# A LayerNorm whose variance ScalarE finishes, and a last down product that takes one half of its columns first

## The chip, the cores and the metric

One core of one Trainium2 chip. The time is the device time of one execution in microseconds (us); the median of several runs is given. The profile shows one further execution.

## What is computed

256 tokens of width 1024 pass through two parts. The first has two layers; each is a feed-forward product with SwiGLU, a mixer (gated linear attention in the first layer, retention in the second) and a second SwiGLU, every one with a residual and a LayerNorm behind it. The second part has one layer: three kinds of attention whose results are gated and merged, a LayerNorm, a feed-forward product with a squared ReLU of hidden width 4096, and the last LayerNorm. That makes eight LayerNorms of this form (the second part's has the same mathematics):

```python
def layer_norm(x, g, b):
    mu = x.mean(-1, keepdims=True)
    var = jnp.square(x - mu).mean(-1, keepdims=True)
    return (x - mu) * lax.rsqrt(var + LN_EPS) * g + b      # LN_EPS = 1e-5

h = jnp.square(jax.nn.relu(x @ w_ff1))
x = layer_norm(alpha * x + h @ w_ff2, ln2_g, ln2_b)        # norm 8, the output
```

All data are fp32 and the products must be good to nearly fp32.

## The kernel before

Every fp32 product is made of three products of split operands: a value is a high part (rounded to the format that TensorE takes at one pass) and a low part (the rest). `three` (L1587 to L1598) issues high by high, high by low and low by high. The weights stream from HBM in tiles of 128 x 2048 through a ring of three slots: SyncE loads `raw`, ScalarE rounds it into `weights_hi` (`split_hi`, L436), VectorE subtracts to get `weights_lo` (`split_lo`, L919), TensorE uses both and gives the slot free (`weights_used`). All engines run programs written out by hand, each in its own order, tied by semaphores that count.

The tokens lie in two row blocks (tb = 0 and 1) of 128 rows. A down product ahead of a norm is summed in four PSUM banks, `acc[:, 2 * tb + half]`, one for each row block and half (512) of the columns. `block_product` (L1770 to L1799) makes the last tiles of such a product: all of row block 0, then all of row block 1. Within a row block it goes through its tiles s, the two chunks of 128 input rows in each tile (k) and the two halves; in the last tile it takes half 0 for both k before half 1. Before norm 8 (final=8, L2305) there are two tiles, so a row block has 24 matmuls, and of them the last 6 are for half 1 and the 6 ahead of these for half 0. When a half is complete it increments `acc_ready`, or `weights_used` for the last one.

Each norm works on these banks, one row block after the other:

- VectorE (`layer_norm`, L937 to L1006) evacuates a half with the residual added and sums it by row (`scalar_tensor_tensor`, L950), forms from half 0's sum a scaled mean (L955), evacuates half 1, and forms the gap of the sums, minus the mean, and `moment[3]` = gap squared minus the first second moment (L962, L963, L965, `surplus_ready`). Then it centres and multiplies by the gain (L970), waits for `rstd_ready`, and normalises the two halves (L975), each of which gives `xn_ready`.
- ScalarE (`layer_norm`, L450 to L474) squares each half about the scaled mean of half 0 and sums by row into `moment[0]` and `moment[1]` (L459), waits through `link` for each, and signals `first_moment` (half 0) and `var_ready` (half 1). In norms 1 to 7 it goes on with weight tiles and with rounding the transposed rows (L448).
- GpSimd (`layer_norm`, L350 to L361) waits for `surplus_ready` and `var_ready`, and in `inverse_root` (L325 to L330) makes moment[1] - moment[3] + eps with a tensor_scalar (L329) and its power of -1/2 with a tensor_tensor (L330). In norms 1 to 7 it also splits half of a weight tile (L338), makes the scaled residual (L348) and loads the next gains and shifts.
- TensorE transposes the normalised rows of norms 1 to 7 (`turn_rows`, L1606) in between its matmuls. Behind norm 8 comes only the output: SyncE stores four pieces (L310) as their `xn_ready` arrives.

VectorE does all of norm 8's row block 0 before anything of row block 1. Small tiles are declared first, then a filler of 24 floats a partition, `to_a_row`, then the large ones (L71 to L101).

Of the kernel before, what the change touches and what calls it, by code (L numbers as in the profile page):

```python
# [9 lines left out]
ALU = mybir.AluOpType  # L10
ACT = mybir.ActivationFunctionType
AX_X = mybir.AxisListType.X

P = 128
D = 1024
TOK = 256
TB = TOK // P
KC = D // P
NCOL = 512
# [18 lines left out]
LN_EPS, NORM_EPS = 1e-5, 1e-6  # L38
# [23 lines left out]
def build(nc, io):  # L62
    ctx = ExitStack()
    with ctx:
        def sb(name, shape, dt=F32, where=ctx):
            return where.enter_context(nc.sbuf_tensor(name, shape, dt))
# [4 lines left out]

        row_sum = sb("row_sum", [P, 2 * TB])
        minus_mean = sb("minus_mean", [P, TB])
        scaled_mean = sb("scaled_mean", [P, TB])
        moment = sb("moment", [P, TB, 4])
        ln_rstd = sb("ln_rstd", [P, TB])
        stats = sb("stats", [P, 8, 6])
# [237 lines left out]
        def _(pool):  # L315
            step = [0]

            def link(ins):
                step[0] += 1
                ins.then_inc(pool_step, 1)  # L320
                pool.wait_ge(pool_step, step[0])

            powers = [0]

            def inverse_root(out, var, scale, eps, n, op=ALU.mult):  # L325

                powers[0] += 1
                pool.wait_ge(var_ready, powers[0])
                link(nc.gpsimd.tensor_scalar(out, var, scale, eps, op, ALU.add))  # L329
                nc.gpsimd.tensor_tensor(out, out, minus_half[:, 0:n], ALU.pow).then_inc(rstd_ready, 1)  # L330

            link(nc.gpsimd.memset(minus_half[:, :], -0.5))

            def split_lo_piece(n, ln):
# [14 lines left out]

            def layer_norm(ln):  # L350
                for tb in range(TB):
                    pool.wait_ge(surplus_ready, 2 * (ln - 1) + tb + 1)
                    inverse_root(ln_rstd[:, tb:tb + 1], moment[:, tb, 1:2], moment[:, tb, 3:4], LN_EPS, 1, ALU.subtract)
                    if ln < 8 and tb == 0:
                        pool.wait_ge(xn_ready, 4 * (ln - 1) + 2)
                        split_lo_piece(LAYER_STARTS[ln] + 1, ln)
                if ln < 8:
                    pool.wait_ge(xn_ready, 4 * ln)
                    for tb in range(TB):
                        residual(tb, ALPHA if ln < 6 else ALPHA_2)  # L360
                    load_rows(ln + 1)  # L361
# [7 lines left out]
            pool.dma_start(cst[:, 1:, :], io["constants"][:, 1:, :]).then_inc(consts_loaded, 16)  # L369
            layer_norm(1)  # L370

            inverse_root(rstd[:, 0:4], g_ss[:, 0:4], 1.0 / GLA_DV, NORM_EPS, 4)
            inverse_root(rstd[:, 4:8], g_ss[:, 4:8], 1.0 / GLA_DV, NORM_EPS, 4)
            layer_norm(2)
            layer_norm(3)
            layer_norm(4)
# [16 lines left out]
                last.then_inc(gate_ready, 1)  # L393

            head_gain(0)
            inverse_root(rstd[:, 0:4], mv[:, 0:4, 1], 1.0, NORM_EPS, 4)
            head_gain(1)
            inverse_root(rstd[:, 4:8], mv[:, 4:8, 1], 1.0, NORM_EPS, 4)
            head_gain(2)
            head_gain(3)  # L400
            layer_norm(5)
# [14 lines left out]
        def _(act):  # L416
            step = [0]

            def link(ins):
                step[0] += 1  # L420
                ins.then_inc(act_step, 1)
                act.wait_ge(act_step, step[0])
# [29 lines left out]
            def layer_norm(ln, end):  # L452

                for tb in range(TB):
                    act.wait_ge(mean_ready, 2 * (ln - 1) + tb + 1)
                    for b in range(2):
                        cols = slice(b * NCOL, (b + 1) * NCOL)
                        act.wait_ge(evacuated, 4 * (ln - 1) + 2 * tb + b + 1)
                        link(nc.scalar.activation(squares[:, cols], xn[:, tb, cols], ACT.Square, bias=scaled_mean[:, tb:tb + 1],  # L459
                                                  scale=D ** -0.5, accum_out=moment[:, tb, b:b + 1]))  # L460
                        act.sem_inc(var_ready if b else first_moment, 1)  # L461
                    if ln == 8:
                        continue
                    if tb == 0 and ln != 2:
                        split_hi(end)
                    if tb == 0 and ln == 2:
                        split_hi(end + 1, first_piece=True)
                    if tb == 1:
                        split_hi(end + 2)
                    rows_hi(f"ln{ln}", tb, block_acc(tb))  # L470
                    if tb == 0 and ln != 2:
                        split_hi(end + 1, first_piece=True)
# [429 lines left out]
        def _(dve):  # L902
# [35 lines left out]
            def layer_norm(ln, end, scale):  # L938

                dve.wait_ge(rows_loaded, 32 * ln)  # L940
                for tb in range(TB):
                    dve.wait_ge(resid_ready, 2 * (ln - 1) + tb + 1)
                    held = ln == 2
                    for b in range(2):
                        cols = slice(b * NCOL, (b + 1) * NCOL)
                        if (tb, b) == (1, 1):
                            dve.wait_ge(weights_used, end)
                        else:
                            dve.wait_ge(acc_ready, 3 * (ln - 1) + 2 * tb + b + 1)
                        nc.vector.scalar_tensor_tensor(  # L950
                            out=xn[:, tb, cols], in0=acc[:, 2 * tb + b, :], scalar=scale, in1=resid[:, tb, cols],
                            op0=ALU.mult, op1=ALU.add, accum_out=row_sum[:, 2 * tb + b:2 * tb + b + 1]).then_inc(evacuated, 1)
                        if b == 0:
                            dve.wait_ge(evacuated, 4 * (ln - 1) + 2 * tb + 1)
                            nc.vector.tensor_scalar(scaled_mean[:, tb:tb + 1], row_sum[:, 2 * tb:2 * tb + 1], -2 * D ** -1.5, None,  # L955
                                                    ALU.mult).then_inc(mean_ready, 1)
                        if held and (tb, b) == (1, 0):
                            rows_lo("ln2", 0, block_acc(0), (0,))
                    dve.wait_ge(evacuated, 4 * (ln - 1) + 2 * tb + 2)
# [21 lines left out]
                    def split_lo_rest(cols):  # L981
                        s = slot_of(end + 1)
                        return nc.vector.tensor_tensor(w_lo[:, s, cols], raw[:, s, cols], w_hi[:, s, cols].bitcast(F32), ALU.subtract)
# [5 lines left out]
                    if held and tb == 1:  # L989
                        rows_lo("ln2", 0, block_acc(0), (1,))  # L990
                    elif ln < 8 and tb == 1:
                        dve.wait_ge(hi_split, end + 2)
                        split_lo_rest(slice(POOL_COLS, POOL_COLS + NCOL))
                    count[0] += 1
                    dve.wait_ge(rstd_ready, count[0])
                    normalise(halves[0])
# [590 lines left out]
        def _(pe):  # L1587
# [23 lines left out]
            def turn_normed(ln, tb):  # L1611
                return turn_rows(f"ln{ln}", xn, tb, block_acc(tb), xn_ready, lambda b: 4 * (ln - 1) + 2 * tb + b + 1)
# [157 lines left out]
            def block_product(n, ready, value, chunks, first=False, final=None, hooks={}):  # L1770

                tiles = len(chunks) // 2
                for tb in range(TB):
                    t = slice(tb * P, (tb + 1) * P)
                    for s in range(tiles):
                        slot = slot_of(n + s)
                        pe.wait_ge(lo_split, n + s + 1)  # L1780
                        pe.wait_ge(ready, value(tb, s))
                        order = [(k, half) for k in range(2) for half in range(2)]
                        if final is not None and s == tiles - 1:
                            order.sort(key=lambda at: at[1])
                        for k, half in order:
                            h_hi, h_lo, c = chunks[2 * s + k]
                            inner = (None, None)
                            if (tb, s, k, half) in hooks:
                                hooks[tb, s, k, half]()
                            if final is not None and final < 8 and (tb, s, k, half) == ((1, 1, 1, 1) if tiles == 2 else (1, 2, 0, 0)):  # L1790
                                inner = turn_normed(final, 0)
                            cols = slice(k * D + half * NCOL, k * D + (half + 1) * NCOL)
                            last = three(acc[:, 2 * tb + half, :], h_hi[:, c, t], h_lo[:, c, t], w_hi[:, slot, cols],
                                         w_lo[:, slot, cols], first and s == 0 and k == 0,
                                         final is not None and s == tiles - 1 and k == 1, inner)
                            if final is not None and s == tiles - 1 and k == 1 and (tb, half) != (1, 1):
                                last.then_inc(acc_ready, 1)
                        if tb == TB - 1:
                            last.then_inc(weights_used, 1)  # L1799

            def turn_hidden(j, cols, banks):
# [624 lines left out]
```

## Time and profile before

| | |
|---|---|
| median of 3 runs | 1522.58 us (1522.49 to 1522.61) |
| the profiled execution: its time | 1522.43 us |
| the profiled execution: its span | 1520.6 us, at a granted clock of 0.999 |
| TensorE, matmuls (PE) | 1512.0 us busy, 99%, 8164 instructions |
| TensorE, weight loads (PEld) | 1300.5 us, 86% |
| VectorE (DVE) | 972.2 us, 64%, 1013 instructions |
| ScalarE (ACT) | 761.6 us, 50%, 756 instructions |
| GpSimd (POOL) | 139.8 us, 9%, 141 instructions |
| DMA | 187 GB/s on average |

A span counts from the first to the last instruction of the trace; the time of the same execution is 1.8 us longer. The engines work at once, so that the busy times do not add up. Matmuls overlap: each lasts some 0.39 us in the timeline, and the next starts 0.23 us after it. A timeline row gives the start, the duration, the engine, the line, the operation and its tiles, and in square brackets how long the engine had been idle and what released it.

### The profile page before, as it was taken

The page shows a single profiled execution, that of the slowest core. Times are in us where ns is not written, and L with a number is a line of the kernel's source. Part 1 is how long each engine was busy: PE and PEld are TensorE (multiplying, and loading weights), DVE is VectorE, ACT ScalarE, POOL GpSimd, SP SyncE. Part 2 cuts the span into 40 slices and gives each one's busy share as a digit, 9 for nine tenths or more (in the row PEclk, how much of TensorE's full clock was granted, in tenths as well). Part 3 has the DMA queues.
Part 4 walks back from the last instruction along what each step waited for, and adds up shares of the span by engine and source line. Part 5 has one row for each costly group of instructions (what it writes and reads, how often), then busy time and mean ns, then how long its engine had stood idle before and what let it go on. Part 6 is the DMA issues. An engine that isn't in the chain of part 4 may idle for free.

```text
span 1520.6 us, 20606 instructions
## 1 busy us (share of the span) xinstructions
PE 1512.0 (99%) x8164; PEld 1300.5 (86%) x8164; DVE 972.2 (64%) x1013; ACT 761.6 (50%) x756; POOL 139.8 (9%) x141
## 2 busy tenths in 40 slices
PE   9999999999999999999999999999999999999998
PEld 8888889888888888888888888888898888888886
DVE  5556576765567556587667655557686556785555
ACT  5454465554545454454434545455536566354442
POOL 1000020100002000024021200002002200020000
PEclk9999999999999999999999999999999999999999
DMA  8554564355544654555544454556444434465551
GB/s 311 196 192 172 214 222 166 131 220 205 192 169 187 227 192 175 211 217 199 175 164 166 173 224 185 185 201 226 166 167 141 162 142 166 166 216 200 191 187 64
DMA packets 42264, 283.71 MB, mean 187 GB/s; under 512 B 5088, under 2 KB 5536, under 8 KB 9552
## 3 DMA queue, kind: packets, MB, share of 16 engines
q1 hardware_dynamic: 38016, 270.55, 48.3%
q0 software_dynamic: 2368, 8.59, 1.7%
q10 hardware_dynamic: 1808, 3.55, 0.6%
q8 instruction: 54, 0.88, 0.2%
q14 instruction: 18, 0.15, 0.0%
HBM read 281.55 MB, written 1.05 MB: 186 GB/s over the span
## 4 chain that ended last, share of the span: by engine, by line
PE 99%; DMA 0%; DVE 0%; ACT 0%; POOL 0%; issue 0%; SPq 0%; DVEq 0%; POOLq 0%; ACTq 0%
PE psum L1699 21%; PE psum L1594 16%; PE psum L1597 16%; PE psum L1598 16%; PE psum L1703 11%; PE psum L1726 5%; PE psum L1733 3%; PE psum L1639 2%; PE psum L1632 2%; PE psum L1626 2%; PE psum L1606 1%; PE psum L2125 0%; DMA weights_raw<-in_weights 0%; PE psum L2088 0%; PE psum L2146 0%; PE psum L1979 0%
## 5 line engine op out<-in xcount | busy, mean ns | idle before, releaser
L919 DVE TENSOR_TENSOR weights_lo<-weights_raw,weights_hi 128x2048 fp32r<-128x2048 f32 x247 | 569.7, 2318 | 318.2 <-ACT weights_hi L436 316.8
L436 ACT ACTIVATE weights_hi<-weights_raw 128x2048 fp32r<-128x2048 f32 (+1 forms) x254 | 479.5, 1890 | 301.2 <-PE psum L1598 144.3
L1699 PE MATMUL psum<-operand,weights_hi 128*128 128x512 f32 x1376 | 327.6, 390 | 0.0
L1699 PEld LDWEIGHTS psum<-operand,weights_hi 128*128 128x128 f32 x1376 | 255.3, 188 | 51.1
L1594 PE MATMUL psum<-weights_hi,hidden_hi 128*128 128x512 f32 x480 | 187.8, 391 | 0.0
L1597 PE MATMUL psum<-weights_lo,hidden_hi 128*128 128x512 f32 x480 | 187.6, 391 | 0.0
L1598 PE MATMUL psum<-weights_hi,hidden_lo 128*128 128x512 f32 x480 | 186.8, 389 | 0.0
L1703 PEld LDWEIGHTS psum<-operand,weights_lo 128*128 128x128 f32 x1376 | 176.4, 191 | 6.7
L1703 PE MATMUL psum<-operand,weights_lo 128*128 128x256 f32 x1376 | 178.5, 283 | 0.0
L1594 PE MATMUL psum<-weights_hi,operand 128*128 128x512 f32 x384 | 151.6, 395 | 0.0
L1597 PE MATMUL psum<-weights_lo,operand 128*128 128x512 f32 x384 | 149.9, 390 | 0.0
L1598 PE MATMUL psum<-weights_hi,operand 128*128 128x512 f32 x352 | 137.2, 390 | 0.0
L1598 PEld LDWEIGHTS psum<-weights_hi,hidden_lo 128*128 128x128 f32 x480 | 90.1, 188 | 18.9
L1594 PEld LDWEIGHTS psum<-weights_hi,hidden_hi 128*128 128x128 f32 x480 | 90.3, 188 | 17.7 <-issue 0.2
L1597 PEld LDWEIGHTS psum<-weights_lo,hidden_hi 128*128 128x128 f32 x480 | 90.3, 188 | 17.0
L329 POOL TENSOR_SCALAR ln_rstd<-moment 128x1 f32<-128x1 f32 x16 | 11.4, 715 | 1013.4 <-ACTq L461 1013.4
L510 ACT ACTIVATE gate_up<-psum 128x512 f32<-128x512 f32 x72 | 39.1, 595 | 128.9 <-PE psum L1703 128.9
L1057 DVE TENSOR_TENSOR gate_up<-psum,gate_up 128x512 f32<-128x512 f32 x72 | 46.4, 686 | 68.0 <-ACT gate_up L510 68.0
L1594 PEld LDWEIGHTS psum<-weights_hi,operand 128*128 128x128 f32 x384 | 72.1, 188 | 15.9 <-issue 1.3
L1597 PEld LDWEIGHTS psum<-weights_lo,operand 128*128 128x128 f32 x384 | 72.2, 188 | 14.2
L1726 PE MATMUL psum<-operand,weights_hi 128*128 128x512 f32 x320 | 80.5, 393 | 0.0
L1598 PEld LDWEIGHTS psum<-weights_hi,operand 128*128 128x128 f32 x352 | 66.1, 188 | 13.8
(299 smaller groups left out, 1844.4 us busy)
## 6 DMA issues: line engine op xcount, KB each, us to landing
weights_raw<-in_weights SPq DMA_DIRECT2D x254, 1024.0 KB, 4.8
ln_rows<-in_ln_rows POOLq DMA_DIRECT2D x16, 512.0 KB, 6.6
weights_raw<-in_weights SPq DMA_DIRECT2D x4, 512.0 KB, 6.6
normalised<-in_x SPq DMA_DIRECT2D x2, 512.0 KB, 6.2
ret_constants<-in_ret_constants ACTq DMA_DIRECT2D x1, 1024.0 KB, 7.7
out<-normalised SPq DMA_DIRECT2D x4, 256.0 KB, 2.0
gla_w_low<-in_gla_w_low ACTq DMA_DIRECT2D x1, 512.0 KB, 5.5
att_w_small<-in_att_w_small ACTq DMA_DIRECT2D x1, 512.0 KB, 5.6
```

Of the source, the lines that this page charges most:

```text
L436: nc.scalar.activation(w_hi[:, s, whole], raw[:, s, whole], ACT.Copy).then_inc(hi_split, 1)
L510: nc.scalar.activation(gate_up[:, at:at + 2, :], against_lo(banks), ACT.Copy).then_inc(against_lo_copied, 1)
L919: nc.vector.tensor_tensor(w_lo[:, s, :], raw[:, s, :], w_hi[:, s, :].bitcast(F32), ALU.subtract).then_inc(lo_split, 1)
L1057: nc.vector.tensor_tensor(gate_up[:, at:at + 2, :], against_hi(banks), gate_up[:, at:at + 2, :], ALU.add).then_inc(up_summed if at else ga ...
L1594: mm(out, a_hi, b_hi, start=start, stop=False, skip_group_check=True)
L1597: mm(out, a_hi, b_lo, start=False, stop=False, skip_group_check=True)
L1598: return mm(out, a_lo, b_hi, start=False, stop=stop, skip_group_check=True)
L1626: mm(out[:, tb, :], x_hi[:, c, t], w_hi[:, slot, cols], start=c == 0, stop=False, skip_group_check=True)
L1699: mm(banks[b // 2][:, b % 2, :], w_hi[:, slot, cols], x_both[:, c, :, :].rearrange("p a t -> p (a t)"), start=c == 0, stop=False, skip_gro ...
L1703: last = mm(banks[b // 2][:, b % 2, 0:TOK], w_lo[:, slot, cols], x_hi[:, c, :], start=False, stop=c == KC - 1, skip_group_check=True)
L1726: mm(banks[half][:, b, :], w_hi[:, slot, cols], x_both[:, c, :, :].rearrange("p a t -> p (a t)"), start=c == 0, stop=False, skip_group_che ...
L1733: last = mm(banks[half][:, b, 0:TOK], w_lo[:, slot, cols], x_hi[:, c, :], start=False, stop=c == KC - 1, skip_group_check=True)
```

## The change

It has three parts. In all eight norms `var_ready` is now signalled by a new ScalarE instruction, an Identity on 128x1 that forms moment[1] - moment[3]; it waits for `surplus_ready`, and GpSimd keeps only the power. The eps enters through the Squares: the scaled mean has two columns, of which the first, used for half 0, has sqrt(eps / 512) added (one VectorE instruction, now with the small new tile `mean_shift` as an operand). In the last down product row block 1 takes half 0 of all its chunks before half 1. And in norm 8 VectorE evacuates half 0 of row block 1 after the centring of row block 0, ahead of the wait for that block's factor.

```diff
-        scaled_mean = sb("scaled_mean", [P, TB])
+        scaled_mean = sb("scaled_mean", [P, TB, 2])
+        mean_shift = sb("mean_shift", [P, 2])
...
-            def inverse_root(out, var, scale, eps, n, op=ALU.mult):
+            def inverse_root(out, n, var=None, scale=1.0, eps=0.0):
...
-                link(nc.gpsimd.tensor_scalar(out, var, scale, eps, op, ALU.add))
+                if var is not None:
+                    link(nc.gpsimd.tensor_scalar(out, var, scale, eps, ALU.mult, ALU.add))
                 nc.gpsimd.tensor_tensor(out, out, minus_half[:, 0:n], ALU.pow).then_inc(rstd_ready, 1)
+            nc.gpsimd.memset(mean_shift[:, 0:1], (LN_EPS / NCOL) ** 0.5)
+            nc.gpsimd.memset(mean_shift[:, 1:2], 0.0)
...
-                    pool.wait_ge(surplus_ready, 2 * (ln - 1) + tb + 1)
-                    inverse_root(ln_rstd[:, tb:tb + 1], moment[:, tb, 1:2], moment[:, tb, 3:4], LN_EPS, 1, ALU.subtract)
+                    inverse_root(ln_rstd[:, tb:tb + 1], 1)
...
-                        link(nc.scalar.activation(squares[:, cols], xn[:, tb, cols], ACT.Square, bias=scaled_mean[:, tb:tb + 1],
+                        link(nc.scalar.activation(squares[:, cols], xn[:, tb, cols], ACT.Square, bias=scaled_mean[:, tb, b:b + 1],
                                                   scale=D ** -0.5, accum_out=moment[:, tb, b:b + 1]))
-                        act.sem_inc(var_ready if b else first_moment, 1)
+                        if b == 0:
+                            act.sem_inc(first_moment, 1)
+                    act.wait_ge(surplus_ready, 2 * (ln - 1) + tb + 1)
+                    nc.scalar.activation(ln_rstd[:, tb:tb + 1], moment[:, tb, 3:4], ACT.Identity, bias=moment[:, tb, 1:2],
+                                         scale=-1.0).then_inc(var_ready, 1)
...
+                        nc.vector.scalar_tensor_tensor(
+                            out=scaled_mean[:, tb, :], in0=row_sum[:, 2 * tb:2 * tb + 1].to_broadcast([P, 2]), scalar=-2 * D ** -1.5,
+                            in1=mean_shift[:, :], op0=ALU.mult, op1=ALU.add).then_inc(mean_ready, 1)
...
-                        if b == 0:
-                            dve.wait_ge(evacuated, 4 * (ln - 1) + 2 * tb + 1)
-                            nc.vector.tensor_scalar(scaled_mean[:, tb:tb + 1], row_sum[:, 2 * tb:2 * tb + 1], -2 * D ** -1.5, None,
-                                                    ALU.mult).then_inc(mean_ready, 1)
+                        if (ln, tb, b) != (8, 1, 0):
+                            evacuate(tb, b)
...
+                    if ln == 8 and tb == 0:
+                        dve.wait_ge(resid_ready, 2 * ln)
+                        evacuate(1, 0)
                     count[0] += 1
                     dve.wait_ge(rstd_ready, count[0])
                     normalise(halves[0])
...
+                    order = [(s, k, half) for s in range(tiles) for k in range(2) for half in range(2)]
+                    if final is not None:
+                        halves_from = 0 if final == 8 and tb else tiles - 1
+                        order.sort(key=lambda at: (min(at[0], halves_from), at[2] if at[0] >= halves_from else 0))
+                    for j, (s, k, half) in enumerate(order):
```

## Rows read from the trace of the kernel before

**Rows 1.** The page of the profile: the span; PE's busy time, share of the span, instructions.

```profile
span 1520.6 us, 20606 instructions
...
PE 1512.0 (99%) x8164; PEld 1300.5 (86%) x8164; DVE 972.2 (64%) x1013; ACT 761.6 (50%) x756; POOL 139.8 (9%) x141
```

**Rows 2.** PE's own waits: us in total, how many, the longest.

```profile
PE psum L1850 <- DVE squares L1080: 1.1, 1, 1.1
```

**Rows 3.** Groups of weight loads in the norms: busy, mean ns, idle before, what ended it.

```profile
L1632 PEld LDWEIGHTS psum<-weights_hi,operand 128*128 128x128 f32 x120 | 22.4, 188 | 5.1 <-DVE operand L935 0.3
L1639 PEld LDWEIGHTS psum<-weights_lo,operand 128*128 128x128 f32 x120 | 21.4, 188 | 4.6 <-DVE weights_lo L983 0.3
L1606 PEld LDWEIGHTS psum<-constants,normalised 128*128 128x128 f32 x128 | 16.2, 145 | 4.1 <-DVE normalised L975 1.0 <-DMA constants<-in_constants 0.3
```

**Rows 4.** The timeline of norm 8, row block 1, to the last normalise.

```profile
1512.78 0.39 PE L1598 MATMUL psum<-weights_hi,hidden_lo 128*128 128x512 f32 x1
...
1513.26 0.15 DVE L955 TENSOR_SCALAR scaled_mean<-row_sum 128x1 f32<-128x1 f32 x1
1513.33 0.68 DVE L950 SCALAR_TENSOR_TENSOR normalised<-psum,residual 128x512 f32<-128x512 f32 x1
...
1514.08 0.19 ACT L459 ACTIVATION_READ_ACCUMULATOR squares<-normalised,scaled_mean 128x1 f32 x1
...
1514.39 0.72 ACT L459 ACTIVATE squares<-normalised,scaled_mean 128x512 f32<-128x512 f32 x1
...
1514.57 1.28 DVE L970 SCALAR_TENSOR_TENSOR residual<-normalised,minus_mean,ln_rows 128x1024 f32<-128x1024 f32 x1
1515.02 0.19 ACT L459 ACTIVATION_READ_ACCUMULATOR squares<-normalised,scaled_mean 128x1 f32 x1
1515.43 0.58 POOL L329 TENSOR_SCALAR ln_rstd<-moment 128x1 f32<-128x1 f32 x1 [4.33 <-ACTq L461]
1516.10 0.57 POOL L330 TENSOR_TENSOR ln_rstd<-ln_rstd,minus_half 128x1 f32<-128x1 f32 x1
...
1516.77 1.41 DVE L975 SCALAR_TENSOR_TENSOR normalised<-residual,ln_rstd,ln_rows 128x512 f32<-128x512 f32 x2 [0.92 <-POOL ln_rstd L330]
```

**Rows 5.** The timeline of norm 8, row block 0.

```profile
1507.34 0.39 PE L1598 MATMUL psum<-weights_hi,hidden_lo 128*128 128x512 f32 x1
...
1507.77 0.69 DVE L950 SCALAR_TENSOR_TENSOR normalised<-psum,residual 128x512 f32<-128x512 f32 x1 [0.38 <-PE psum L1598]
...
1508.50 0.72 ACT L459 ACTIVATE squares<-normalised,scaled_mean 128x512 f32<-128x512 f32 x1 [0.26 <-DVE normalised L950]
...
1509.01 1.28 DVE L970 SCALAR_TENSOR_TENSOR residual<-normalised,minus_mean,ln_rows 128x1024 f32<-128x1024 f32 x1
...
1509.54 0.91 POOL L329 TENSOR_SCALAR ln_rstd<-moment 128x1 f32<-128x1 f32 x1 [162.66 <-ACTq L461]
...
1511.21 1.41 DVE L975 SCALAR_TENSOR_TENSOR normalised<-residual,ln_rstd,ln_rows 128x512 f32<-128x512 f32 x2 [0.92 <-POOL ln_rstd L330]
```

**Rows 6.** The timelines of VectorE and GpSimd in norm 1 and in norm 2, row block 1.

```profile
195.05 0.69 DVE L983 TENSOR_TENSOR weights_lo<-weights_raw,weights_hi 128x512 fp32r<-128x512 f32 x1
...
195.27 0.90 POOL L330 TENSOR_TENSOR ln_rstd<-ln_rstd,minus_half 128x1 f32<-128x1 f32 x1
...
298.38 0.69 DVE L935 TENSOR_TENSOR operand<-psum,operand 128x512 fp32r<-128x512 f32 x1
...
298.60 0.57 POOL L330 TENSOR_TENSOR ln_rstd<-ln_rstd,minus_half 128x1 f32<-128x1 f32 x1
```

**Rows 7.** Groups of ScalarE by form: the narrowest activation, and table loads.

```profile
L721 ACT ACTIVATE att_p<-att_p,att_max 128x128 f32<-128x128 f32 x16 | 6.2, 392 | 2.5 <-DVE att_max L1355 2.5
...
L766 ACT ACT_TABLE_LOAD x3 | 3.8, 1283 | 0.1
```

**Rows 8.** Groups of VectorE by form, 128x1536 with two inputs in SBUF.

```profile
L1389 DVE TENSOR_TENSOR att_p<-att_pT,att_p 128x1536 f32<-128x1536 f32 x2 | 3.5, 1756 | 0.0
L1394 DVE TENSOR_TENSOR att_logs_lo<-att_p,att_logs_hi 128x1536 fp32r<-128x1536 f32 x2 | 3.5, 1753 | 0.0
```

More of the change, by code:

```diff
@@ L370, in _ @@
             layer_norm(1)
-            inverse_root(rstd[:, 0:4], g_ss[:, 0:4], 1.0 / GLA_DV, NORM_EPS, 4)
-            inverse_root(rstd[:, 4:8], g_ss[:, 4:8], 1.0 / GLA_DV, NORM_EPS, 4)
+            inverse_root(rstd[:, 0:4], 4, g_ss[:, 0:4], 1.0 / GLA_DV, NORM_EPS)
+            inverse_root(rstd[:, 4:8], 4, g_ss[:, 4:8], 1.0 / GLA_DV, NORM_EPS)
             layer_norm(2)
@@ L395, in _ @@
             head_gain(0)
-            inverse_root(rstd[:, 0:4], mv[:, 0:4, 1], 1.0, NORM_EPS, 4)
+            inverse_root(rstd[:, 0:4], 4, mv[:, 0:4, 1], 1.0, NORM_EPS)
             head_gain(1)
-            inverse_root(rstd[:, 4:8], mv[:, 4:8, 1], 1.0, NORM_EPS, 4)
+            inverse_root(rstd[:, 4:8], 4, mv[:, 4:8, 1], 1.0, NORM_EPS)
             head_gain(2)
@@ L940, in layer_norm, with evacuate @@
                 dve.wait_ge(rows_loaded, 32 * ln)
+                def evacuate(tb, b):
+                    cols = slice(b * NCOL, (b + 1) * NCOL)
+                    if (tb, b) == (1, 1):
+                        dve.wait_ge(weights_used, end)
+                    else:
+                        dve.wait_ge(acc_ready, 3 * (ln - 1) + 2 * tb + b + 1)
+                    nc.vector.scalar_tensor_tensor(
+                        out=xn[:, tb, cols], in0=acc[:, 2 * tb + b, :], scalar=scale, in1=resid[:, tb, cols],
+                        op0=ALU.mult, op1=ALU.add, accum_out=row_sum[:, 2 * tb + b:2 * tb + b + 1]).then_inc(evacuated, 1)
+                    if b == 0:
+                        dve.wait_ge(evacuated, 4 * (ln - 1) + 2 * tb + 1)
+                        nc.vector.scalar_tensor_tensor(
+                            out=scaled_mean[:, tb, :], in0=row_sum[:, 2 * tb:2 * tb + 1].to_broadcast([P, 2]), scalar=-2 * D ** -1.5,
+                            in1=mean_shift[:, :], op0=ALU.mult, op1=ALU.add).then_inc(mean_ready, 1)
                 for tb in range(TB):
@@ L944, in layer_norm @@
                     for b in range(2):
[L945 to L952, printed above, removed]
-                        if b == 0:
-                            dve.wait_ge(evacuated, 4 * (ln - 1) + 2 * tb + 1)
-                            nc.vector.tensor_scalar(scaled_mean[:, tb:tb + 1], row_sum[:, 2 * tb:2 * tb + 1], -2 * D ** -1.5, None,
-                                                    ALU.mult).then_inc(mean_ready, 1)
+                        if (ln, tb, b) != (8, 1, 0):
+                            evacuate(tb, b)
                         if held and (tb, b) == (1, 0):
@@ L1777, in block_product @@
                     t = slice(tb * P, (tb + 1) * P)
-                    for s in range(tiles):
-                        slot = slot_of(n + s)
[L1780 to L1798, printed above, removed]
@@ new lines, in block_product @@
+                    order = [(s, k, half) for s in range(tiles) for k in range(2) for half in range(2)]
[3 more added lines that the diff above has]
+                    for j, (s, k, half) in enumerate(order):
+                        slot = slot_of(n + s)
+                        if j == 0 or s > max(at[0] for at in order[:j]):
+                            pe.wait_ge(lo_split, n + s + 1)
+                            pe.wait_ge(ready, value(tb, s))
+                        h_hi, h_lo, c = chunks[2 * s + k]
+                        inner = (None, None)
+                        if (tb, s, k, half) in hooks:
+                            hooks[tb, s, k, half]()
+                        if final is not None and final < 8 and (tb, s, k, half) == ((1, 1, 1, 1) if tiles == 2 else (1, 2, 0, 0)):
+                            inner = turn_normed(final, 0)
+                        cols = slice(k * D + half * NCOL, k * D + (half + 1) * NCOL)
+                        last = three(acc[:, 2 * tb + half, :], h_hi[:, c, t], h_lo[:, c, t], w_hi[:, slot, cols],
+                                     w_lo[:, slot, cols], first and s == 0 and k == 0,
+                                     final is not None and s == tiles - 1 and k == 1, inner)
+                        if final is not None and s == tiles - 1 and k == 1 and (tb, half) != (1, 1):
+                            last.then_inc(acc_ready, 1)
+                        if tb == TB - 1 and s not in [at[0] for at in order[j + 1:]]:
```

## The prediction

> **What bounds the kernel now.** I read the page first: the span is 1520.6 us, and TensorE's matmul side is busy for 1512.0 of it, 99% [rows 1]. A change on another engine can therefore bring something in two places only: where PE waits for it, and after PE's last matmul. The waits say how much there is of the first: PE itself waited once, 1.1 us, for a memset at the start [rows 2]. Its weight loads waited 1.0 us in six places at the transposes for the normalised rows, 0.3 us for an operand and 0.3 us for a piece of a split weight tile [rows 3]; all three belong to the norms' stages, so about 1.6 us is everything that seven norms could give back. The second place is the tail, which only norm 8 has. There the timeline shows every step [rows 4]: the last matmul starts at 1512.78, the normalise of the last row block at 1516.77, and the span ends at 1520.6.
>
> **The tail of before, step by step.** In row block 0 the last matmul starts at 1507.34 and the evacuation that needs it at 1507.77, 0.43 later [rows 5]. In row block 1 the same distance would give 1512.78 + 0.43 = 1513.21, but the evacuation starts at 1513.33, because VectorE still had the mean of the first half to do (1513.26): 0.12 us late. In block 0 the Square of the second half follows its evacuation after 0.73 us (1507.77 to 1508.50) [rows 5]; in block 1 it follows after 1.06 (1513.33 to 1514.39), because the Square of the first half had only just been read out (1514.08 + 0.19): 0.33 us late [rows 4]. Then the read-out (1515.02 + 0.19 = 1515.21), GpSimd's tensor_scalar at 1515.43, its power at 1516.10, finished at 1516.67, and the normalise at 1516.77 [rows 4].
>
> **Part 1: the last product takes its first half of columns first.** Block 1 of the product has 24 matmuls; 1512.78 - 1507.34 over 24 is 0.227 us each. The first half is now complete after 12 of them instead of 18: its last matmul starts at 1507.34 + 12 x 0.227 = 1510.06, so VectorE may evacuate at 1510.49. That is after its centring of block 0 (1509.01 + 1.28 = 1510.29) [rows 5], and with the small mean it is through by about 1511.4. The normalise of block 0 (before at 1511.21) starts some 0.1 to 0.2 us later and is done by 1512.8, before 1513.21. So the second half is evacuated at 1513.21, and ScalarE's first Square is long finished: both lags go, 0.12 and 0.33. PE's own work costs nothing more: the same matmuls, one weight load each, and no wait of the block is later than it was, for both tiles were already used by block 0. The stores of block 0 leave up to 0.2 us later; before, both its halves were ready at 1511.21 + 1.41 = 1512.62 [rows 5], so 7.8 us of span cover them.
>
> **Part 2: ScalarE's Identity for GpSimd's tensor_scalar.** Removed from each of 16 row blocks is a GpSimd instruction, in the tail 1515.43 to 1516.10, 0.67 us [rows 4]. Added is one ScalarE instruction on 128x1, for which before has no row. Below it lies the read-out of an accumulator on 128x1, 0.19 us [rows 4]; above it the 128x128 activation, 0.39 us [rows 7]. I take 0.30 and keep both ends. Its new wait is for VectorE's small product, which precedes the centring (1514.57 before, so ready by then) and so ends before the last Square is read out: it costs nothing there. By these terms: Square at 1513.21 + 0.73 = 1513.94, read-out from 1514.57 to 1514.76, Identity from 1514.88 (0.12 after, as between 1514.27 and 1514.39) to 1515.18, power from 1515.28.
>
> **Part 3: what the power then meets.** GpSimd does not run freely beside VectorE. In block 0 of norm 8 the tensor_scalar starts at 1509.54 and lasts 0.91, to 1510.45: 0.16 after the end of the centring (1510.29) that runs beside it [rows 5]. In block 1 it ends at 1516.01, 0.16 after 1514.57 + 1.28 = 1515.85 [rows 4]. The power shows the same in norm 1, where it starts beside a split of two SBUF tiles (195.05 + 0.69 = 195.74), takes 0.90 instead of 0.57, and ends at 196.17, 0.43 after it; in norm 2 it runs beside an operation with only one input from SBUF (298.38 to 299.07) and takes its 0.57 [rows 6]. The centring has two tiles from SBUF. It would start at 1513.21 + 1.24 = 1514.45 (the distance from evacuation to centring is 1.24 in both blocks) and end at 1515.73. So the power that is ready at 1515.28 ends not at 1515.85 but at 1515.73 + 0.43 = 1516.16, and the normalise starts 0.10 later, at 1516.26. Against 1516.77 this is a gain of 0.51 us. The Identity is thereby covered: the power may be ready 0.31 us later (1516.16 - 0.57 = 1515.59) before anything moves, so either end of its price gives the same sum. Without that cover each 0.1 us of it would be 0.1 us of the end.
>
> The Trainium skill, "SBUF — State Buffer", section "Who interferes with whom", has the lock: a VectorE instruction with two SBUF inputs keeps GpSimd's reads out for its whole length. Its probe figure, about 115 ns after VectorE's end, is for descriptors; read as the power starting whole after the centring it would give 1515.73 + 0.57 + 0.10 = 1516.40 and a gain of 0.37 us. The measured end, 0.43 after, decides.
>
> **Part 4: norms 1 to 7.** The first blocks get their factor up to 0.4 us sooner, but PE reaches the transposes of block 0 in its own order, without a wait, and VectorE's next steps wait for PE. In the second blocks the power would be ready at about 195.1, beside the split that starts at 195.05, and would end at 196.17 as before [rows 6]. ScalarE gets 14 Identities of some 0.4 us with their gaps; behind them are its weight splits and the rounding of the transposed rows, for which it then waits for PE. Nothing of it is on PE's path: 0. The two memsets on GpSimd, two columns instead of one in the mean, and the argument order of the other powers lie beside matmuls: 0.
>
> **The sum.** The profiled execution took 1522.43 us; 1522.43 - 0.51 = 1521.92. The median of the runs is 1522.58, 0.15 above that execution, so I forecast 1522.1 for the median. The bound that a measurement can tell is 0.2%, here 3.0 us: this is no change that can be told.
>
> **Rivals.** (a) The power is not held by the centring: it ends at 1515.85, the normalise starts at 1515.95, gain 0.82, time 1521.6 to 1521.8. Against it are the rows on both blocks and on norm 1. 8%. (b) The sooner factors also reach PE and take away its 1.6 us [rows 3]: 0.51 + 1.6 gives 1520.3 to 1520.5. Against it: those waits are for VectorE's normalise of the second block, whose factor stays at the same time by part 4. 5%. (c) The end on the other side: the change adds a small tile ahead of the filler "to_a_row" and leaves the filler as it is, so every large tile starts some bytes later. If a matmul then took one clock more, 0.42 ns at 2.4 GHz, 8164 of them [rows 1] would cost 3.4 us: 1525.5. It decides from 0.37 ns a matmul on. Before has tiles that by their declared sizes start off a boundary of 512 bytes, att_logs_hi among them, and VectorE's operation on it takes 1753 ns beside 1756 for the same shape on aligned ones [rows 8]; no row shows the very offset on PE. 3%. (d) Identity loads a table. A load takes 1.283 us [rows 7]; in the tail the power would be ready at 1516.56, the normalise at 1517.23, a loss of 0.46 in place of the gain; in seven norms it would push ScalarE's rounding past its idle 1.1 us, up to 1.8 each for two loads, so 1523 to 1535. There is no load at the Square's or the Copy's lines, which come right after Silu. 2%.
>
> The Trainium skill, "ScalarE: Activation LUTs", section "Table sets: the hidden batching unit", says that cheap functions, identity among them, are in every set; by that rule (d) doesn't occur, and no row here can show it for Identity.
>
> **How the numbers follow.** My forecast holds 82%, its own range 1521.6 to 1522.5, from its bounds and the scatter of the runs. (a) and (b) are on the same side and within 3.0 us, so "faster" by over 0.2% keeps only 0.02. "Slower" has (c), (d) and whatever I don't see: 0.06. The range has to leave out at most 2 in 10; it reaches to 1521.2, which takes in (a), and upward to 1523.1, for a median 0.05% off between sessions.
>
> **What would show it.** In the profile after: the evacuation of the last half 0.43 us after the last matmul's start; the last Square 0.73 us after it; one Identity of 0.2 to 0.4 us; a power that lasts some 0.9 us instead of 0.57 and ends 0.43 after the centring; the normalise 3.5 us after the last matmul's start instead of 4.0; PE's waits in the norms as before. The prediction is wrong if PE's matmuls stand further apart than 0.227 us, if a table load stands before an Identity, or if the last power takes 0.57 us beside the centring.

## The result: 8.1 us slower, and the profile after

The changed kernel takes 1530.6 us (median of 5 runs, 1530.52 to 1530.65) against 1522.5 us before (5 runs, 1522.37 to 1522.61). The ratio is 1.0053 with a 95% interval of 1.0042 to 1.0064. The forecast was 1522.1 us in a range of 1521.2 to 1523.1, with 6% for a loss of over 0.2%.

The page of the changed kernel, its first lines and the shares of the chain that ended last:

```profile
span 1528.7 us, 20592 instructions
...
PE 1513.7 (99%) x8164; PEld 1299.8 (85%) x8164; DVE 982.6 (64%) x1013; ACT 765.8 (50%) x772; POOL 132.5 (9%) x127
...
PE 93%; DVE 3%; ACT 2%; issue 1%; POOL 0%; DMA 0%; POOLq 0%; SPq 0%; DVEq 0%; ACTq 0%
```

The span is 8.1 us longer than in [rows 1]. PE is busy 1.7 us longer, and of the chain it has 93% where it had 99% before: the chain now leaves it for VectorE, ScalarE and "issue". PE's own waits (us in total, how many, the longest), of which before had only the one in [rows 2]:

```profile
PE psum L1622 <- DVE normalised L988: 6.0, 6, 1.2
...
PE psum L1648 <- DVE operand L942: 0.6, 2, 0.4
```

Six waits for the normalised rows, 6.0 us, and two for an operand (a further one of 0.2 us, for a high part of a weight tile, lies in the first 14 us): the norms have to do with it, not the tail. The last matmul starts at 1521.25 and did at 1512.78 [rows 4], 8.47 us later, and matmul by matmul the two traces drift apart in seven steps, one of 0.96 to 1.45 us at each of norms 1 to 7, and by 0.1 us at most outside them. The timeline of norm 1, row block 1, shows one such step, here in the changed kernel:

```profile
192.04 2.40 POOL L342 TENSOR_TENSOR weights_lo<-weights_raw,weights_hi 128x1024 fp32r<-128x1024 f32 x1 [5.29 <-ACT weights_hi L437]
...
192.66 1.80 DVE L960 SCALAR_TENSOR_TENSOR scaled_mean<-row_sum,mean_shift 128x2 f32<-128x2 f32 x1
...
194.38 0.68 DVE L955 SCALAR_TENSOR_TENSOR normalised<-psum,residual 128x512 f32<-128x512 f32 x1
...
194.49 0.72 ACT L462 ACTIVATE squares<-normalised,scaled_mean 128x512 f32<-128x512 f32 x1 [1.65 <-DVE scaled_mean L960]
...
196.39 0.69 DVE L996 TENSOR_TENSOR weights_lo<-weights_raw,weights_hi 128x512 fp32r<-128x512 f32 x1
...
196.64 0.85 POOL L332 TENSOR_TENSOR ln_rstd<-ln_rstd,minus_half 128x1 f32<-128x1 f32 x1 [2.21 <-ACT ln_rstd L467]
...
197.53 0.75 DVE L988 SCALAR_TENSOR_TENSOR normalised<-residual,ln_rstd,ln_rows 128x512 f32<-128x512 f32 x1 [0.45 <-POOL ln_rstd L332]
...
198.33 0.65 PE L1622 MATMUL psum<-constants,normalised 128*128 128x128 f32 x4 [0.96 <-DVE normalised L988]
```

GpSimd splits its half of a weight tile from 192.04 to 194.44. VectorE's new mean, two elements a partition, starts inside at 192.66 and ends at 194.46: 1.80 us for work that takes 0.16 elsewhere, and it ends with GpSimd's instruction. In all seven norms it ends 0.02 us after the split does. The evacuation behind it on VectorE starts 1.6 us later than before, ScalarE's Square, which waits for the mean, 1.7 us later, and PE waits 0.96 us for the normalised rows. The same stretch of the kernel before:

```profile
191.94 2.40 POOL L338 TENSOR_TENSOR weights_lo<-weights_raw,weights_hi 128x1024 fp32r<-128x1024 f32 x1 [4.89 <-ACT weights_hi L434]
...
192.61 0.15 DVE L955 TENSOR_SCALAR scaled_mean<-row_sum 128x1 f32<-128x1 f32 x1
...
193.51 0.21 DVE L962 TENSOR_SCALAR moment<-row_sum 128x1 f32<-128x1 f32 x1
...
193.88 0.47 DVE L965 SCALAR_TENSOR_TENSOR moment<-moment 128x1 f32<-128x1 f32 x1
...
196.21 0.75 DVE L975 SCALAR_TENSOR_TENSOR normalised<-residual,ln_rstd,ln_rows 128x512 f32<-128x512 f32 x1 [0.46 <-POOL ln_rstd L330]
...
197.01 0.46 PEld L1606 LDWEIGHTS psum<-constants,normalised 128*128 128x128 f32 x4 [0.16 <-DVE normalised L975]
...
197.11 0.60 PE L1606 MATMUL psum<-constants,normalised 128*128 128x128 f32 x4
```

The old mean ran in the middle of the same split, in 0.15 us. The normalise was done at 196.96, and PE's weight load for the transposes, which starts at 197.01, had already waited 0.16 us for it. So the stage had no slack: what VectorE loses here, PE loses. The new mean takes 1.6 us more than the old one, the normalise comes 1.32 us later (197.53 for 196.21; the sooner factor gives back the rest), and as the changed kernel is 0.10 us behind before this norm, some 1.2 us of that are new. PE's step at this norm is 1.19 us.

The tail of the changed kernel answers to [rows 4]:

```profile
1521.25 0.39 PE L1614 MATMUL psum<-weights_hi,hidden_lo 128*128 128x512 f32 x1
...
1521.75 0.69 DVE L955 SCALAR_TENSOR_TENSOR normalised<-psum,residual 128x512 f32<-128x512 f32 x1 [0.47 <-PE psum L1614]
...
1522.49 0.72 ACT L462 ACTIVATE squares<-normalised,scaled_mean 128x512 f32<-128x512 f32 x1 [1.68 <-DVE normalised L955]
...
1522.99 1.28 DVE L983 SCALAR_TENSOR_TENSOR residual<-normalised,minus_mean,ln_rows 128x1024 f32<-128x1024 f32 x1
...
1523.33 0.29 ACT L467 ACTIVATE ln_rstd<-moment 128x1 f32<-128x1 f32 x1
...
1523.70 0.98 POOL L332 TENSOR_TENSOR ln_rstd<-ln_rstd,minus_half 128x1 f32<-128x1 f32 x1 [4.53 <-ACT ln_rstd L467]
...
1524.79 1.42 DVE L988 SCALAR_TENSOR_TENSOR normalised<-residual,ln_rstd,ln_rows 128x512 f32<-128x512 f32 x2 [0.51 <-POOL ln_rstd L332]
```

From the last matmul's start to the normalise it is 3.54 us now and was 3.99; from that start to the end of the span it is 7.45 and was 7.82. So 8.47 us lost in the norms and 0.37 won in the tail are the 8.1 us.

### The profile page after: what moved, and what is told of

Its sections match the earlier page's. It is cut to its first block, busy times and chain, and to the rows that moved or that the text cites. A ratio compares the mean times of both kernels' runs of the same rounds, so it can differ in the third digit from the quotient of the medians.

```text
span 1528.7 us, 20592 instructions
## 1 busy us (share of the span) xinstructions
PE 1513.7 (99%) x8164; PEld 1299.8 (85%) x8164; DVE 982.6 (64%) x1013; ACT 765.8 (50%) x772; POOL 132.5 (9%) x127
## 4 chain that ended last, share of the span: by engine, by line
PE 93%; DVE 3%; ACT 2%; issue 1%; POOL 0%; DMA 0%; POOLq 0%; SPq 0%; DVEq 0%; ACTq 0%
PE psum L1715 20%; PE psum L1610 16%; PE psum L1613 15%; PE psum L1614 15%; PE psum L1719 11%; PE psum L1742 5%; PE psum L1749 2%; PE psum L1655 1%; PE psum L1648 1%; PE psum L1642 1%; DVE weights_lo L926 1%; DVE scaled_mean L960 1%; ACT weights_hi L439 1%; ACT squares L462 1%; PE psum L1622 1%
## 5 line engine op out<-in xcount | busy, mean ns | idle before, releaser
L332 POOL TENSOR_TENSOR ln_rstd<-ln_rstd,minus_half 128x1 f32<-128x1 f32 x16 | 15.3, 954 | 1027.5 <-ACT ln_rstd L467 1027.5
```

## The experiments

**Theory.** VectorE's new mean cannot run beside GpSimd's weight split, since it needs what the split holds. The expectations call this the port theory, after the way into SBUF that the two engines would share. **Rivals.** The placement of the tiles; ScalarE's Identity and its new wait, which may delay ScalarE's work for the norms; the mean's own form (two columns, a broadcast).

**e1_two_scalars**, the change with another way to the same two columns:

```diff
-nc.vector.scalar_tensor_tensor(out=scaled_mean[:, tb, :], in0=row_sum[...].to_broadcast([P, 2]), scalar=-2 * D ** -1.5,
-                               in1=mean_shift[:, :], op0=ALU.mult, op1=ALU.add)
+nc.vector.tensor_scalar(scaled_mean[:, tb, 0:1], row_sum[...], -2 * D ** -1.5, (LN_EPS / NCOL) ** 0.5, ALU.mult, ALU.add)
+nc.vector.tensor_scalar(scaled_mean[:, tb, 1:2], row_sum[...], -2 * D ** -1.5, None, ALU.mult)
```

> The changed kernel, but the two columns of the scaled mean come from two small tensor_scalars with one input each (immediates for the scale and the eps term), in place of one instruction with two inputs from SBUF. Port theory (the two-input mean waits until GpSimd's weight split of 2.40 us ends, in norms 1 to 7, row block 1): each of these takes 0.15 us again, PE's wait for the normalised rows of 6.0 us goes, and only the tail's gain stays: 1522.0 to 1522.3. Rival, ScalarE (the Identity and its wait for the surplus delay ScalarE's other work in the norms): about 1530.6, as before the edit. Rival, placement of the tiles: 1530.6 too, since the small tile stays.

Measured: 1521.41 us, against 1522.43 before on the same chip; ratio 0.9993 (0.9984 to 1.0003). The whole loss is gone with this one instruction, and the Identity, its wait and the small tile are still there. Its timeline of norm 1, row block 1:

```profile
191.93 2.41 POOL L342 TENSOR_TENSOR weights_lo<-weights_raw,weights_hi 128x1024 fp32r<-128x1024 f32 x1 [5.30 <-ACT weights_hi L437]
...
192.54 0.15 DVE L960 TENSOR_SCALAR scaled_mean<-row_sum 128x1 f32<-128x1 f32 x1
...
192.61 0.14 DVE L962 TENSOR_SCALAR scaled_mean<-row_sum 128x1 f32<-128x1 f32 x1
...
194.94 0.56 POOL L332 TENSOR_TENSOR ln_rstd<-ln_rstd,minus_half 128x1 f32<-128x1 f32 x1 [0.60 <-ACT ln_rstd L467]
...
195.05 0.69 DVE L997 TENSOR_TENSOR weights_lo<-weights_raw,weights_hi 128x512 fp32r<-128x512 f32 x1
...
195.66 0.74 DVE L989 SCALAR_TENSOR_TENSOR normalised<-residual,ln_rstd,ln_rows 128x512 f32<-128x512 f32 x1
...
197.10 0.60 PE L1623 MATMUL psum<-constants,normalised 128*128 128x128 f32 x4
```

The means take 0.15 and 0.14 us inside the split. The result is 0.6 us better than I expected: PE's last matmul starts at 1512.12, 0.66 us sooner than before. The power shows why: it starts at 194.94, ahead of VectorE's split at 195.05, and takes 0.56 us; before it came at 195.27 and took 0.90 [rows 6]. The normalise moves from 196.21 to 195.66. Of the small waits of [rows 3] those for the normalised rows and for the split piece go; the 0.3 us for an operand stay.

**e2_before_two_inputs**, the kernel before with a mean of one column and two inputs:

```diff
-nc.vector.tensor_scalar(scaled_mean[:, tb:tb + 1], row_sum[...], -2 * D ** -1.5, None, ALU.mult)
+nc.vector.scalar_tensor_tensor(out=scaled_mean[:, tb:tb + 1], in0=row_sum[...], scalar=-2 * D ** -1.5,
+                               in1=mean_shift[:, 0:1], op0=ALU.mult, op1=ALU.add)      # mean_shift is zero
```

> The kernel before with one edit: the scaled mean (one column) is made by a scalar_tensor_tensor with a tile of zeros as its second SBUF input, in place of the tensor_scalar. Port theory: the seven means of row block 1 in norms 1 to 7 last 1.7 to 1.9 us instead of 0.15 and PE loses about 1.2 us in each: 1522.5 + 8.5 = 1531.0. Rival, ScalarE: 1522.5, for there is no Identity. Rival, the two-column broadcast: 1522.5, for there is one column.

Measured: 1533.55 us, ratio 1.0073 (1.0056 to 1.0089). The group of the mean (busy us, mean ns):

```profile
L957 DVE SCALAR_TENSOR_TENSOR scaled_mean<-row_sum,mean_shift 128x1 f32<-128x1 f32 x16 | 13.8, 863 | 0.6
```

Seven of the sixteen are long (1.74 to 1.84 us). The loss is 11.1 us, more than the changed kernel's 8.1: in the changed kernel the Identity, which spares GpSimd an instruction, gives back some 0.4 us in each norm once the factor is on PE's path (the first normalise of norm 1's row block 1 starts at 197.94 in e2 and at 197.53 in the changed kernel), and 0.4 in the tail. I had not counted that.

**e3_before_two_columns**, the kernel before with one input and two columns:

```diff
-nc.vector.tensor_scalar(scaled_mean[:, tb:tb + 1], row_sum[:, 2 * tb:2 * tb + 1], -2 * D ** -1.5, None, ALU.mult)
+nc.vector.tensor_scalar(scaled_mean[:, tb, :], row_sum[:, 2 * tb:2 * tb + 1].to_broadcast([P, 2]), -2 * D ** -1.5, None, ALU.mult)
```

> The kernel before with the scaled mean written as two columns from a broadcast of the sum, by a tensor_scalar with one SBUF input. Port theory (two inputs are what matters): 0.15 to 0.16 us each and 1522.5. Rival, the form (two columns or the broadcast cost something or take the port): some of the seven means are long and the time is up to 1531.

Measured: 1533.43 us, ratio 1.0072 (1.0055 to 1.0089). My theory in its first form, that the second input matters, missed this one:

```profile
L955 DVE TENSOR_SCALAR scaled_mean<-row_sum 128x2 f32<-128x2 f32 x16 | 14.0, 872 | 0.6
```

One input is held just as long when there are two elements. Either property of the new mean was enough.

**e9_two_plain_columns** takes the broadcast away: the sums' tile gets a second, zero column beside each sum.

```diff
+nc.vector.tensor_scalar(scaled_mean[:, tb, :], row_sum[:, 2 * tb, :], -2 * D ** -1.5, None, ALU.mult)
```

> As e3_before_two_columns, but the two elements that the one-input tensor_scalar reads are two neighbouring columns of the sums' tile (the second holds zero), so that nothing is broadcast. If two elements in SBUF are enough for the instruction to need GpSimd's port: seven means of 1.8 us and 1533.4, as with the broadcast. If the broadcast did it: 0.15 to 0.17 us each and 1522.4.

Measured: 1533.58 us, ratio 1.0073 (1.0055 to 1.0092), with the same group:

```profile
L955 DVE TENSOR_SCALAR scaled_mean<-row_sum 128x2 f32<-128x2 f32 x16 | 13.9, 868 | 0.6
```

So it is the second element. The Trainium skill, "VectorE: DVE Perf Modes", section "What auto-detection actually checks", says that VectorE takes its mode 2×_2P (the page's name for the use of both read ports for one tensor) if a single source and the destination are in SBUF and their outermost dimensions longer than one are both even or equal; two columns fulfil this, and one column has no such dimension. The runs agree with it (1.85 us at most with two columns in e3 and e9, 0.15 with one in e1); that the mode itself was entered, no trace shows.

**e4_before_placement** moves all large tiles as far as the change does, by an unused tile `sb("more_ahead", [P, 2])` ahead of the filler (32 bytes in both kernels).

> The kernel before with one unused small tile ahead of the filler, so that all large tiles start as many bytes later as in the changed kernel. Port theory: placement plays no part, 1522.5. Rival of the prediction, placement (0.42 ns a matmul): 1525.9, or up to all of the loss, 1530.6.

Measured: 1522.40 against 1522.43 us, ratio 1.0000 (0.9990 to 1.0009). Placement plays no part.

**e5_short_split** changes the other side of the collision, with the mean of the changed kernel as it is: `POOL_COLS = 512` for 1024.

> The changed kernel with GpSimd's piece of the weight split cut from 1024 to 512 columns (VectorE's last piece grows by 512). Port theory: the split lasts about 1.2 us instead of 2.40 and starts some 0.4 us sooner, so that it is over within 0.2 us of the mean's start; the seven means last 0.2 to 0.4 us instead of 1.8, PE's wait for normalised rows falls from 6.0 us to under 1.5, and the time to 1521.4 to 1524. Rival, ScalarE or the mean's own form: means as long as before the edit, 1530.6 or more.

Measured: 1524.04 us, 0.04 above the upper end of what I expected; ratio 1.0011 (1.0000 to 1.0021). Norm 1:

```profile
191.43 1.29 POOL L342 TENSOR_TENSOR weights_lo<-weights_raw,weights_hi 128x512 fp32r<-128x512 f32 x1 [4.87 <-ACT weights_hi L437]
...
192.47 0.27 DVE L960 SCALAR_TENSOR_TENSOR scaled_mean<-row_sum,mean_shift 128x2 f32<-128x2 f32 x1
```

The split ends at 192.72, and the mean, started at 192.47, ends at 192.74. Six of the seven means last 0.26 to 0.27 us. The seventh, in norm 2, starts 0.57 us after its split and lasts 0.73, more than I expected, and it too ends 0.02 us after the split. PE's waits for normalised rows are gone; what is left is of another kind, seven waits for the larger last piece that VectorE now splits:

```profile
PE psum L1655 <- DVE weights_lo L996: 1.4, 7, 0.4
```

**e6_norms_1_to_3** is e1_two_scalars with the changed kernel's mean in norms 1, 2 and 3.

> As e1_two_scalars, but norms 1, 2 and 3 keep the two-input mean of the changed kernel. Port theory: the loss is a sum over norms; the traces of the changed kernel and of e1_two_scalars stand 1.3, 1.0 and 1.3 us apart on PE in these three, so 1521.4 + 3.6 = 1525.0. If the loss came once, or only with all of them, 1521.4 or 1530.6.

Measured: 1524.95 us; ratio 1.0017 (1.0006 to 1.0028). The loss adds up norm by norm.

**e7_identity_alone** and **e8_order_alone** take the parts of the change singly. In e7 `halves_from = tiles - 1` everywhere and VectorE evacuates in the old order, with the two scalar means and the Identity; in e8 GpSimd has its tensor_scalar back, ScalarE no Identity, and the mean is one column from one input, as before.

> The kernel before with ScalarE's Identity alone (the two small scalar forms of the mean; the last product and VectorE's order in norm 8 as before). With the power held by the centring: Square at 1514.39 as before, Identity ready by 1515.65, power held until 0.41 after 1515.85, normalise 0.40 earlier than before; PE gains its 0.66 us in norms 1 to 7 as in e1_two_scalars: 1522.4 - 1.06 = 1521.4, so that the order of the last product is worth nothing on top. Rival, the parts add up (0.45 from the order): 1521.8.

> The kernel before with the order of the last product and VectorE's early evacuation alone (GpSimd keeps its tensor_scalar). With GpSimd held by the centring: the Square comes 0.4 us sooner, but the tensor_scalar ends 0.16 us after the centring whenever it comes, which moves by 0.05 to 0.12 us only: 1522.3 to 1522.4. Rival, the parts add up: 1522.0 (0.45 us less).

Measured: e7 1521.32 us (ratio 0.9993, 0.9982 to 1.0003), e8 1522.47 us (ratio 1.0000, 0.9990 to 1.0011), before 1522.43. The tail of e7, then that of e8:

```profile
1512.28 0.39 PE L1612 MATMUL psum<-weights_hi,hidden_lo 128*128 128x512 f32 x1
...
1513.94 1.28 DVE L984 SCALAR_TENSOR_TENSOR residual<-normalised,minus_mean,ln_rows 128x1024 f32<-128x1024 f32 x1
...
1514.77 0.86 POOL L332 TENSOR_TENSOR ln_rstd<-ln_rstd,minus_half 128x1 f32<-128x1 f32 x1 [4.56 <-ACT ln_rstd L467]
...
1515.73 1.41 DVE L989 SCALAR_TENSOR_TENSOR normalised<-residual,ln_rstd,ln_rows 128x512 f32<-128x512 f32 x2 [0.51 <-POOL ln_rstd L332]
```

```profile
1512.88 0.39 PE L1610 MATMUL psum<-weights_hi,hidden_lo 128*128 128x512 f32 x1
...
1514.62 1.28 DVE L979 SCALAR_TENSOR_TENSOR residual<-normalised,minus_mean,ln_rows 128x1024 f32<-128x1024 f32 x1
...
1515.15 0.92 POOL L331 TENSOR_SCALAR ln_rstd<-moment 128x1 f32<-128x1 f32 x1 [3.95 <-ACTq L465]
...
1516.82 1.42 DVE L984 SCALAR_TENSOR_TENSOR normalised<-residual,ln_rstd,ln_rows 128x512 f32<-128x512 f32 x2 [0.92 <-POOL ln_rstd L332]
```

In both GpSimd's instruction that runs beside the centring ends 0.41 us (power, e7) or 0.17 us (tensor_scalar, e8) after it: 1513.94 + 1.28 + 0.41 = 1515.63 and 1514.62 + 1.28 + 0.17 = 1516.07. The earlier Square of e8 brings GpSimd's start to 2.27 us after the last matmul's, from 2.65 [rows 4], and GpSimd only waits longer: from the last matmul's start to the normalise it is 3.94 us, against 3.99 before and 3.45 in e7. The order of the last product is worth nothing here.

**e10_gain_in_psum** and **e11_identity_gain_in_psum** test the lock in the tail by taking its cause away, on e1 and on e7:

```diff
+# ScalarE, ahead of norm 8
+act.wait_ge(rows_loaded, 32 * 8)
+nc.scalar.activation(work[:, 0:2, :], by_half(ln_rows[:, 0, :]), ACT.Copy).then_inc(gain_copied, 1)
...
-                            in1=ln_rows[:, 0, cols], op0=ALU.add, op1=ALU.mult))
+                            in1=work[:, 0:2, :], op0=ALU.add, op1=ALU.mult))        # norm 8 only
```

> As e1_two_scalars, but in norm 8 the centring takes the gain from PSUM (ScalarE copies it there in its idle time before the norm), so that it has one input from SBUF. Port theory: the last power is no longer held, takes 0.56 us instead of 0.97, and the last normalise starts about 0.4 us sooner, 3.1 us after the last matmul's start: 1521.4 - 0.4 = 1521.0. If the power's length had another cause (a first instruction after idle time): 0.97 us again and 1521.4.

> As e7_identity_alone (order of the last product as before) with the gain in PSUM for norm 8 as well. Port theory: the power, ready at 1514.77 of that trace, takes 0.56 instead of 0.86 and the normalise starts 0.3 us sooner, 3.15 us after the last matmul's start: 1521.3 - 0.3 = 1521.0. Freed of the lock, the order of the last product should be worth something at last: e10_gain_in_psum would be ahead of this one by up to 0.3 us less the 0.08 that its evacuation starts later.

Measured: e10 1520.85 us and e11 1520.81 us, both with ratio 0.9990 (0.9981 to 0.9999) to before. e10:

```profile
1512.09 0.39 PE L1627 MATMUL psum<-weights_hi,hidden_lo 128*128 128x512 f32 x1
...
1513.84 1.27 DVE L992 SCALAR_TENSOR_TENSOR residual<-normalised,minus_mean,psum 128x1024 f32<-128x1024 f32 x1
...
1514.55 0.55 POOL L333 TENSOR_TENSOR ln_rstd<-ln_rstd,minus_half 128x1 f32<-128x1 f32 x1 [4.95 <-ACT ln_rstd L468]
...
1515.20 1.41 DVE L1001 SCALAR_TENSOR_TENSOR normalised<-residual,ln_rstd,ln_rows 128x512 f32<-128x512 f32 x2
```

The centring with one input from SBUF lasts 1.27 us as ever, and the power beside it takes 0.55 instead of 0.97; so its length in e1 was a wait for the centring, and not that of a first instruction after idle time. In e11 the normalise comes 3.03 us after the last matmul's start, in e10 3.11:

```profile
1512.13 0.39 PE L1624 MATMUL psum<-weights_hi,hidden_lo 128*128 128x512 f32 x1
...
1515.16 1.41 DVE L1001 SCALAR_TENSOR_TENSOR normalised<-residual,ln_rstd,ln_rows 128x512 f32<-128x512 f32 x2
```

My expectation that the order of the product would now be ahead by up to 0.2 us failed: in e10 the last evacuation starts 0.50 us after the last matmul's start, in e11 0.43, and with VectorE free sooner e11's last Square follows its evacuation by 0.73 us all the same, so that no lag was left to remove. Why the evacuation starts 0.07 us later behind twelve matmuls into the same bank is open.

## Why the prediction was wrong, point by point

- **The step that failed is in part 4**: "The two memsets on GpSimd, two columns instead of one in the mean, and the argument order of the other powers lie beside matmuls: 0." The mean's new form was priced by its own 0.15 us, with matmuls as cover, and never laid beside GpSimd's timeline. Either property of the form costs 11.0 to 11.2 us on the kernel before (e2, e3, e9), and in the changed kernel the form costs 9.2 us (1530.6 against e1's 1521.41).
- **Part 3 had the mechanism and applied it one way.** The rows showed GpSimd held by VectorE. The Trainium skill, "SBUF — State Buffer", section "Who interferes with whom", says that whichever starts first has the port for its whole instruction and the other waits; the trace after agrees for the split (to 194.44) and the mean (to 194.46), though not for every small pair (last section). I had read the section for the power alone. The longest GpSimd instruction of each norm, the split of 2.40 us, was not among my rows. Before, VectorE's small product of two inputs (L965) had a median of 220 ns; in the six norms where it started inside the split it took 475 to 487 ns, and in norm 1 it ended within 0.02 us of the split's end (193.88 + 0.47 and 191.94 + 2.40): the warning was there.
- **What else stood in the norms.** I took 0 as if this work had cover. [rows 3] said otherwise: PE's weight loads already waited for VectorE's normalise, some 0.17 us in each of six norms, and for its operand in another. VectorE's chain was PE's limit there, with no slack at all, and the prediction used these rows only as a bound on what could be gained.
- **The tail (parts 1 to 3) held.** Forecast: normalise 3.48 us after the last matmul, measured 3.54; power held to 0.43 after the centring, measured 1523.70 + 0.98 - 1522.99 - 1.28 = 0.41; Identity 0.30 us, measured 0.29; gain 0.51, measured 0.45 to the normalise and 0.37 to the end of the span. The last evacuation was forecast 0.43 us after the last matmul's start and came after 0.50: that is the 0.06 between 3.48 and 3.54.
- **How its gain divides was only half seen.** The forecast named both lags and the lock. The runs show that the lock makes them overlap: the Identity alone has all of the gain, the order alone none (e7, e8).
- **Rival (b)**, that the sooner factor reaches PE, had 5% and is true in part once the mean is mended: 0.66 us in e1, 0.50 in e7 (which is 0.20 us behind before norm 1, so that its norms give 0.70), of the 1.6. I had argued that the power would end at the same time since it would meet VectorE's split; it is ready 0.11 us ahead of it (194.94 and 195.05) and isn't held.
- **Rivals (a), (c) and (d)** did not occur: the power was held, e4 excludes placement, and no table load stands at the Identities' line (15 loads in the whole trace, as before). The side of (c) was right for a cause that I did not have.

## What to carry to other kernels

Lay every new VectorE instruction, the smallest too, beside the GpSimd instructions of its stretch: with two inputs in SBUF, or with one input and two elements, it waited here for a GpSimd instruction of 2.4 us to end, and one element from one input did not. Price an added operation by its form and neighbours, not by its own duration, and look at the waits of the weight loads too before calling a stage covered: where they already wait for it, it has no slack. Where the lock decides, an earlier input gives nothing; moving one input to PSUM gave 0.5 us.

## What the runs showed that I had not expected

- A tensor_scalar on 128x2 took up to 1.85 us beside GpSimd's split and one on 128x1 0.15 us, in the same place and with the same input.
- A second operand with one value a partition did not make VectorE wait: the gap of the sums (L962), a tensor_scalar on 128x1 that takes the other sum as its scalar, took 0.21 us in the middle of the split, as everywhere.
- The lock worked both ways in one stretch: GpSimd held VectorE's mean to 0.02 us after its own end (194.44 and 194.46), and VectorE held the power to 0.41 us after its.
- Which of the two starts first in the profile does not always say who waits. In norm 1 of e1 the power starts at 194.94, 0.08 us before VectorE's centring ends and 0.11 before its two-input split, and neither was held (0.56 and 0.69 us). In norm 4 of the changed kernel the power starts at 672.53 and VectorE's split at 672.54, and it is the power that waits: it takes 1.11 us and ends 0.41 after the split. Why is not shown, and the profile gives GpSimd's spans only roughly.
